# Weights of the first two lanes requested in the routing stage, and the gate row applied by VectorE as the experts' rows leave PSUM

## The chip, the cores and the metric

One Trainium2 chip, one core. The metric is the device time of one execution in microseconds; the median of three executions of the kernel before is 2322.79 us. All data are float32.

## The reference

Two transformer blocks run one after the other on 512 tokens of width 1024. The change touches only the end of the second, its mixture of experts:

```python
scores = sigmoid(hf @ router_w)                     # 512 tokens x 64 experts
choice = scores + router_bias                       # best 4 of 8 groups, then the best 8 experts
gw = scores[top_e] / sum * 2.5
y[token] += swiglu(hf[token], exp_gate[e], exp_up[e], exp_down[e]) * gw      # 8 experts per token
moe = y + swiglu(hf, sh_gate, sh_up, sh_down)       # the shared expert
x = x + g2 * moe                                    # g2: the gate row, 1024 numbers
return rms_norm_2(x, final_g)
```

An expert has a gate and up matrix of 1024x256 each ("gu", 2.10 MB together) and a down matrix of 256x1024 ("down", 1.05 MB). How many tokens an expert gets is known only once the routing has run.

## The kernel before

The program is a list of phases; each is a block in which the five engines run their own instruction streams, and the next block begins when all engines have left the last one. Three phases matter.

**Routing** (`phase_route`). VectorE works through a chain of some 200 small operations, each waiting for the one before. It picks each token's 8 experts (until L2635), assigns experts to blocks of 128 rows (until L2710, `guests_done`), computes each token's place (`slot_f`, L2732 to L2754), then the two rows of numbers from which the weights are fetched: `K.source[:, 0]`, the block's own expert (L2758 to L2763), and `K.source[:, 1]`, a "visitor" expert that uses 32 of the block's 128 rows (L2765 to L2775). After these it builds one-hot tables `within` (L2787, four operations of 128x1024) and `place` (L2790, 32 operations of 128x96), from which TensorE makes the token lists (L2557). Beside that the shared expert runs: TensorE multiplies gate and up (L2522) and down (L2565, eight products of 128x512, through PSUM banks 6 and 7 in turn), ScalarE copies each product out (L2581), and GpSimd adds them to the residual `K.res` (L2591). GpSimd has multiplied the shared down matrix with the gate row before (L2588).

**Experts** (`phase_experts`). 42 blocks are worked off in 14 trips of three lanes (0, 1, 2). Each lane has one buffer for gu and one for down, each with room for an own expert and a visitor. GpSimd gathers the tokens' rows (L2982) and the weights (L2994) by indirect DMA; a lane's gu buffer is refilled once the gu products of its last block are done, the down buffer once its down products are. GpSimd's order at the start is: rows of block 0, weights of lane 0, rows of block 1, a wait for `weigh_step` (12 operations of VectorE, L2966 to L2968), rows of block 2, weights of lane 1, rows of block 3, weights of lane 2, and so on. Nothing is fetched where the block's expert is that of the lane's block before. VectorE transposes the rows (L2947, 16 operations a block); TensorE multiplies gu (L2872 and L2874), then the down product of the block before, then transposes the hidden rows (L2906). ScalarE makes the silu (L2921), VectorE multiplies with the up half (L2958). The finished block leaves PSUM by halves: ScalarE copies columns 0 to 511 (L2916), VectorE columns 512 to 1023 (L2953); SyncE stores it to `expert_out`.

**Combine** (`phase_combine`). Per token 8 rows of `expert_out` are gathered by 32 indirect DMAs (L3050), one for each of 4 token tiles and 8 choices, into 16 buffers. VectorE sums three of the eight with their weights (L3078, L3076), TensorE the other five through diagonal matrices into PSUM (L3063). VectorE adds both sums (L3081), multiplies with the gate row (L3084), adds the residual (L3085), and the final norm follows: ScalarE squares (L3099) and takes the root (L3101), VectorE scales (L3090).

## Time and profile before

| | us |
|---|---|
| median of three executions (2322.01 to 2322.91) | 2322.79 |
| the profiled execution's own time | 2324.35 |
| its span, first to last instruction | 2322.0 |
| TensorE matmul busy | 2089.7 (90%) |
| VectorE busy | 1276.3 (55%) |
| ScalarE busy | 450.4 (19%) |
| GpSimd busy | 428.5 (18%) |
| mean granted TensorE clock | 0.958 |

The routing lies at about 1609 to 1688 us of the span, the experts at 1688 to 2256, the combine at 2256 to 2322. A time in a row is microseconds from the start of the span. Idle time ahead of an instruction stands in brackets with what ended it; idle time of an engine that nobody waits for costs nothing.

### The profile page before, as it was taken

The page shows a single profiled execution, that of the slowest core. Times are in us where ns is not written, and L with a number is a line of the kernel's source. Part 1 is how long each engine was busy: PE and PEld are TensorE (multiplying, and loading weights), DVE is VectorE, ACT ScalarE, POOL GpSimd, SP SyncE. Part 2 cuts the span into 40 slices and gives each one's busy share as a digit, 9 for nine tenths or more (in the row PEclk, how much of TensorE's full clock was granted, in tenths as well). Part 3 has the DMA queues.
Part 4 walks back from the last instruction along what each step waited for, and adds up shares of the span by engine and source line. Part 5 has one row for each costly group of instructions (what it writes and reads, how often), then busy time and mean ns, then how long its engine had stood idle before and what let it go on. Part 6 is the DMA issues. An engine that isn't in the chain of part 4 may idle for free. (4 is left out here: it accounts for less than half of the span.)

```text
span 2322.0 us, 32745 instructions
## 1 busy us (share of the span) xinstructions
PE 2089.7 (90%) x12785; PEld 1214.8 (52%) x12786; DVE 1276.3 (55%) x2404; ACT 450.4 (19%) x889; POOL 428.5 (18%) x779
## 2 busy tenths in 40 slices
PE   6999999999999999999978999898748889989866
PEld 3444564787786448884453598545423333332322
DVE  3347872666663124433977433434865666767635
ACT  1013562212211011002335323101000011101111
POOL 0005000112000000000000000000154555556525
PEclk9999999999999999999989999998879999999988
DMA  9412000545524114991102100401079999998967
GB/s 386 188 65 99 37 1 3 234 147 215 218 96 169 54 63 157 399 363 70 46 1 111 56 2 3 182 37 64 0 322 379 379 424 406 360 402 329 412 270 313
DMA packets 71163, 433.13 MB, mean 187 GB/s; under 512 B 16227, under 2 KB 16883, under 8 KB 46993
## 3 DMA queue, kind: packets, MB, share of 16 engines
q0 software_dynamic: 39488, 245.00, 26.6%
q1 hardware_dynamic: 31570, 186.65, 20.8%
q8 instruction: 76, 1.25, 0.2%
q14 instruction: 29, 0.24, 0.0%
HBM read 462.47 MB, written 68.73 MB: 229 GB/s over the span
## 5 line engine op out<-in xcount | busy, mean ns | idle before, releaser
L2872 PE MATMUL psum<-arena 128*32 128x512 f32 x3024 | 464.3, 618 | 80.8 <-DMA arena<-in_exp_gu,arena 79.9
L2874 PE MATMUL psum<-arena 128*32 x1008 | 463.3, 618 | 0.0
L965 PE MATMUL psum<-arena 128*128 128x256 f32 x1904 | 416.9, 381 | 3.3 <-PEq L1005 2.0
L965 PEld LDWEIGHTS psum<-arena 128*128 128x128 f32 x1904 | 361.3, 190 | 64.2 <-issue 15.3
L2947 DVE STREAM_TRANSPOSE arena<-arena 32x256 f32<-32x256 f32 x688 | 299.6, 435 | 17.8 <-DMA arena<-scratch_h,arena 9.0
L2872 PEld LDWEIGHTS psum<-arena 128*32 128x32 f32 x3024 | 131.6, 114 | 331.6 <-issue 310.9
L1067 PE MATMUL psum<-arena 128*128 128x512 f32 x352 | 151.8, 592 | 0.3 <-PEq L1091 0.3
L2874 PEld LDWEIGHTS psum<-arena 128*32 128x32 f32 x1008 | 110.8, 113 | 7.2 <-issue 3.5
L869 PE MATMUL psum<-arena 128*128 128x512 f32 x256 | 111.2, 593 | 2.3 <-DVE arena L2432 1.5
L1067 PEld LDWEIGHTS psum<-arena 128*128 128x128 f32 x352 | 66.6, 190 | 83.4 <-issue 83.4
L420 DVE SCALAR_TENSOR_TENSOR arena<-arena 128x512 f32<-128x512 f32 x120 | 94.8, 834 | 5.8 <-PEq L456 4.5
L2921 ACT ACTIVATE arena<-psum 128x256 f32<-128x256 f32 x42 | 16.1, 384 | 394.2 <-PE psum L2874 394.2
L2994 POOL DMA_INDIRECT arena<-in_exp_gu,arena x84 | 84.9, 1011 | 37.0 <-issue 37.0
L2994 POOL DMA_INDIRECT arena<-in_exp_down,arena x84 | 85.1, 1013 | 34.9 <-issue 34.9
L2953 DVE COPY arena<-psum 128x512 f32<-128x512 f32 x42 | 29.1, 692 | 109.7 <-PE psum L2874 109.7
L869 PEld LDWEIGHTS psum<-arena 128*128 128x128 f32 x256 | 48.1, 190 | 61.2 <-issue 58.9
L1200 DVE SCALAR_TENSOR_TENSOR arena<-arena 128x511 f32<-128x511 f32 x88 | 68.2, 774 | 15.9 <-ACT arena L1164 13.6
L1164 ACT ACTIVATE arena<-arena 128x512 f32<-128x512 f32 x44 | 33.5, 807 | 217.4 <-DVE arena L984 217.4
L1600 PE MATMUL psum<-arena 128*128 128x512 f32 x128 | 66.6, 652 | 9.1 <-ACT arena L1700 7.1
L244 PE MATMUL psum<-arena 128*32 128x512 f32 x384 | 51.3, 656 | 25.8 <-DMA arena<-in_w_ada 25.8
L972 DVE TENSOR_TENSOR arena<-arena,psum 128x512 f32<-128x512 f32 x34 | 23.4, 687 | 88.8 <-PE psum L965 88.8
L978 DVE TENSOR_TENSOR arena<-arena,psum 128x512 f32<-128x512 f32 x34 | 23.4, 688 | 83.3 <-PE psum L965 83.2
(572 smaller groups left out, 2929.9 us busy)
## 6 DMA issues: line engine op xcount, KB each, us to landing
scratch_expert_out<-arena SPq DMA_DIRECT2D x18, 2048.0 KB, 19.9
arena<-in_w_ada SPq DMA_DIRECT2D x12, 2048.0 KB, 16.8
arena<-in_ada_w POOLq DMA_DIRECT2D x12, 2048.0 KB, 8.1
arena<-in_w_up SPq DMA_DIRECT2D x22, 1024.0 KB, 4.8
scratch_expert_out<-arena SPq DMA_DIRECT2D x42, 512.0 KB, 7.7
arena<-in_w_in SPq DMA_DIRECT2D x9, 2048.0 KB, 11.3
arena<-in_w_down SPq DMA_DIRECT2D x5, 2048.0 KB, 7.8
arena<-in_w_o SPq DMA_DIRECT2D x2, 2048.0 KB, 8.0
```

Source lines behind the costliest of these rows:

```text
L244: last = pe.matmul(bank[32 * j:32 * j + 32, :], vec[:, k, :], w[:, 512 * k:512 * k + 512], start=(r == 0), stop=(r == 1))
L420: K.tap.by(dve.scalar_tensor_tensor(out=conv[:, k, :], in0=x, scalar=w, in1=conv[:, k, :], op0=ALU.mult, op1=ALU.add))
L869: last = pe.matmul(K.bank[2 * t + half], lhs[:, k, P * t:P * t + P], row(k)[:, 512 * half:512 * half + 512], start=(k == 0), stop=(k == pe ...
L965: last = pe.matmul(out, w[:, k, :], x[:, k, :], start=(k == 0), stop=(k == KH - 1))
L1067: out = pe.matmul(K.bank[2 * t + half], K.hmid[:, k, P * t:P * t + P], w[:, k % 4, 512 * half:512 * half + 512], start=(first and k == inn ...
L1164: seed.by(act.activation(conv(n)[half], rows(n)[:, half, :], ACT.Identity, bias=taps[:, n, 4 * half + 3:4 * half + 4], scale=taps[:, n, 4 ...
L1200: link(dve, dve.scalar_tensor_tensor(out=c[:, to], in0=u[:, fr], scalar=taps[:, n, 4 * half + tap:4 * half + tap + 1], in1=c[:, to], op0=A ...
L1600: last = pe.matmul(K.bank[6 if m == 0 else 7], K.gw[:, m % 2, P * k:P * k + P], K.h[:, k, :], start=(k == 0), stop=(k == KD - 1))
L2872: pe.matmul(bank[r, :], left[:, r], weights[:, OWN, col:col + 512], start=first, stop=last_)
L2874: return pe.matmul(bank[0:GUEST, :], left[:, 0:GUEST], picked, start=first, stop=last_)
L2947: last = dve.transpose(channels[c:c + 32, :, a:a + 32], tokens[a:a + 32, :, c:c + 32])
L2994: pool.indirect_dma_start(to[s][:, who, :], None, src, offset, bounds_check=EXPERTS * P - 1, oob_is_err=False).then_inc(landed_[s].sem, 16)
```

## The change

- In the routing VectorE computes the own experts' numbers right behind `guests_done`, then the shared expert's product for half 0, the first part of the ranks, the product for half 1, the visitors' numbers, and only then the places. TensorE's turned table of block experts (`eb_t`) goes to bank 2 and ahead of the last gate-and-up product.
- GpSimd requests the weights of lanes 0 and 1, own experts and then visitors, eight indirect DMAs in all, as soon as the numbers are there; lane 1 waits for the last gate-and-up product, whose buffers it takes. Down buffers of lanes 1 and 2 now lie in the two weight-stream buffers. In the experts' phase GpSimd's order begins with rows of blocks 0 and 1, the same wait for `weigh_step`, rows of blocks 2 and 3, then weights of lane 2.
- The shared expert's eight down products use six banks; VectorE adds each from PSUM to the residual (eight operations of 128x512). ScalarE's eight copies and GpSimd's four adds are gone.
- `place` is made by four operations of 128x768 on VectorE, and scaled by the token numbers in four operations of ScalarE, where 32 operations did both.
- The gate row for the shared expert is loaded in the phase before.
- In the experts' phase VectorE moves both halves out, each multiplied with a gate row loaded at the phase's start; ScalarE moves none.
- In the combine VectorE sums its three rows straight onto the residual and adds the PSUM sum: three operations of one kind and one of another per tile, where there were six. The gate row's load is gone.

```diff
+            K.gate_in.by(pool.dma_start(K.row[:, 3, :], d["mod_rows"][3].partition_broadcast(P)), 16)
...
-    shared, gate_row = sb("shared", [P, NT, D]), sb("route_gate_row", [P, D])
+    down_at = K.ws_taken + 1
+    gate_up_ws, shared_down_ws = K.ws[:, 1 - down_at % 2, :], K.ws[:, down_at % 2, :]
+    K.memory.release("h")
+    K.e_gu = [None] * UNROLL
+    for lane in (1, 0):
+        K.e_gu[lane] = sb(f"e_gu{lane}", [P, 2, KD * 2 * E_FF])
+    K.e_down = [sb("e_down0", [P, 2, 2 * D])] + [x.rearrange("p (w n) -> p w n", w=2) for x in (gate_up_ws, shared_down_ws)]
+    K.e_gu_in, K.e_down_in = ([sig(f"{n}{s}") for s in range(UNROLL)] for n in ("e_gu_landed", "e_down_landed"))
+    gate_row = K.row[:, 3, :]
...
+            eb_t.by(pe.matmul(K.bank[2][:, P:2 * P], K.ones[:, :], diag[:, :], start=True, stop=True))
...
-            for n in range(2 * NT):
+            def down_products(n):
                 t, half = divmod(n, 2)
-                if n >= 2:
-                    pe.wait_ge(sh_out.sem, n - 1)
+                if n == 5:
+                    pe.wait_ge(ranks_read.sem, 1)
+                if n >= len(down_banks):
+                    pe.wait_ge(added.sem, n - len(down_banks) + 1)
                 for k in range(2):
-                    last = pe.matmul(K.bank[6 + n % 2], act_h[:, k, P * t:P * t + P], w[:, k, 512 * half:512 * half + 512], start=(k == 0), stop=(k == 1))
+                    last = pe.matmul(K.bank[down_banks[n % len(down_banks)]], act_h[:, k, P * t:P * t + P], w[:, k, 512 * half:512 * half + 512], start=(k == 0), stop=(k == 1))
                 dn_mm.by(last)
+
+            for n in range(6):
+                down_products(n)
+            list_products(0)
+            list_products(1)
+            down_products(6)
+            down_products(7)
             free(K, dn_mm)
-            for t in range(NT):
-                last = list_products(t)
-            list_mm.by(last)
+            list_products(2)
+            list_mm.by(list_products(3))
...
-            for n in range(2 * NT):
-                t, half = divmod(n, 2)
-                act.wait_ge(dn_mm.sem, n + 1)
-                sh_out.by(act.activation(shared[:, t, 512 * half:512 * half + 512], K.bank[6 + n % 2], ACT.Copy))
+            for t in range(NT):
+                act.wait_ge(matched.sem, t + 1)
+                numbered.by(act.activation(place[:, t, :, :], place[:, t, :, :], ACT.Copy, scale=const[:, RC_TOKEN + t:RC_TOKEN + t + 1]))
 
         @block.gpsimd
         def _(pool):
+            gu_rows, down_rows = d["exp_gu"].rearrange("e p n -> (e p) n"), d["exp_down"].rearrange("e p n -> (e p) n")
+
+            def fetch(lane, who):
+                row = bass.IndirectOffsetOnAxis(ap=K.source[:, who, LANE * lane:LANE * lane + 1], axis=0)
+                for to, src, landed in ((K.e_gu, gu_rows, K.e_gu_in), (K.e_down, down_rows, K.e_down_in)):
+                    landed[lane].by(pool.indirect_dma_start(to[lane][:, who, :], None, src, row, bounds_check=EXPERTS * P - 1, oob_is_err=False), 16)
+
             pool.wait_ge(K.ws_landed[down_at % 2].sem, 16 * (down_at // 2 + 1))
-            pool.wait_ge(gate_in.sem, 16)
+            pool.wait_ge(K.gate_in.sem, 16)
             for k in range(2):
-                gated.by(pool.tensor_tensor(shared_down[:, k, :], shared_down[:, k, :], gate_row[:, :], ALU.mult))
-            for t in range(NT):
-                pool.wait_ge(sh_out.sem, 2 * t + 2)
-                added.by(pool.tensor_tensor(K.res[:, t, :], K.res[:, t, :], shared[:, t, :], ALU.add))
+                gated.by(pool.tensor_tensor(shared_down[:, k, :], shared_down[:, k, :], gate_row, ALU.mult))
+            pool.wait_ge(own_ready.sem, 1)
+            fetch(0, 0)
+            pool.wait_ge(gu_mm.sem, 4)
+            fetch(1, 0)
+            pool.wait_ge(guest_ready.sem, 1)
+            fetch(0, 1)
+            fetch(1, 1)
...
+            at_first = lambda ap: ap[:, 0:BLOCKS].rearrange("p (l t) -> p l t", l=UNROLL)[:, :, 0]
+            dve.wait_ge(eb_t.sem, 1)
+            step(dve.tensor_copy(src_f[:, :], K.bank[2][:, P:2 * P]))
+            step(tt(again[:, 1:P], src_f[:, 1:P], src_f[:, 0:P - 1], ALU.is_equal))
+            step(dve.memset(at_first(again), 0.0))
+            step(ts(at_first(src_f), at_first(src_f), EXPERTS - 1.0, None, ALU.min))
+            step(ts(src_f[:, :], src_f[:, :], float(P), const[:, RC_ROW:RC_ROW + 1], ALU.mult, ALU.add))
+            link(dve, stt(out=K.source[:, 0, :], in0=again[:, 0:BLOCKS], scalar=NOWHERE, in1=src_f[:, 0:BLOCKS], op0=ALU.mult, op1=ALU.add), own_ready)
+
             def shared_product(m):
                 dve.wait_ge(sg_act.sem, m + 1)
                 dve.wait_ge(gu_mm.sem, m + 3)
                 sh_mul.by(tt(act_h[:, m, :], hg[:, m, :], K.bank[6 + m], ALU.mult))
+
+            shared_product(0)
...
+            shared_product(1)
...
+            link(dve, stt(out=K.source[:, 1, :], in0=again[:, 0:BLOCKS], scalar=NOWHERE, in1=src_f[:, 0:BLOCKS], op0=ALU.mult, op1=ALU.add), guest_ready)
...
+            link(dve, tt(tmp[:, :, :], rank, spread_e(limit), ALU.is_ge), ranks_read)
...
+            def add_shared(n):
+                t, half = divmod(n, 2)
+                x = K.res[:, t, 512 * half:512 * half + 512]
+                dve.wait_ge(dn_mm.sem, n + 1)
+                added.by(tt(x, x, K.bank[down_banks[n % len(down_banks)]], ALU.add))
+
             for t in range(NT):
-                low = part[:, 0, TOP * t:TOP * t + TOP].unsqueeze(2).to_broadcast([P, TOP, P])
-                step(tt(within[:, t, :, :], count.unsqueeze(1).to_broadcast([P, TOP, P]), low, ALU.is_equal))
-                for j in range(TOP):
-                    n = TOP * t + j
-                    last = ts(place[:, t, j, :], count[:, 0:BLOCKS], part[:, 1, n:n + 1], const[:, RC_TOKEN + t:RC_TOKEN + t + 1], ALU.is_equal, ALU.mult)
-                    if j < TOP - 1:
-                        r_step.by(last)
-                dve.wait_ge(r_step.sem, r_step.n)
-                link(dve, last, hot)
+                low, high = (part[:, a, TOP * t:TOP * t + TOP].unsqueeze(2).to_broadcast([P, TOP, n]) for a, n in ((0, P), (1, BLOCKS)))
+                link(dve, tt(place[:, t, :, :], count[:, 0:BLOCKS].unsqueeze(1).to_broadcast([P, TOP, BLOCKS]), high, ALU.is_equal), matched)
+                link(dve, tt(within[:, t, :, :], count.unsqueeze(1).to_broadcast([P, TOP, P]), low, ALU.is_equal), hot)
+                if t == 1:
+                    add_shared(0)
+                    add_shared(1)
+            for n in range(2, 2 * NT):
+                add_shared(n)
...
-                act.activation(out[:, (s - 1) % U, 0:512], K.bank[5], ACT.Copy).then_inc(out_act.sem, 1)
...
-                dve.tensor_copy(out[:, (s - 1) % U, 512:D], K.bank[6]).then_inc(out_dve.sem, 1)
+                if isinstance(i, int) and i == 0 and s == 1:
+                    dve.wait_ge(gate_in.sem, 16)
+                for half in range(2):
+                    last = dve.tensor_tensor(out[:, (s - 1) % U, 512 * half:512 * half + 512], K.bank[5 + half], gate[:, 512 * half:512 * half + 512], ALU.mult)
+                last.then_inc(out_dve.sem, 1)
...
-                if isinstance(i, int) and i + s == 0:
-                    weights(i, s)
-                    gather(i, s, 1)
-                else:
-                    if isinstance(i, int) and i == 0 and s == 1:
-                        pool.wait_ge(weigh_step.sem, 3 * NT)
-                        link(pool, pool.memset(xg[U - 1], 0.0), cleared)
-                    gather(i, s, 1)
+                if isinstance(i, int) and i == 0 and s == 1:
+                    pool.wait_ge(weigh_step.sem, 3 * NT)
+                    link(pool, pool.memset(xg[U - 1], 0.0), cleared)
+                gather(i, s, 1)
+                if not (isinstance(i, int) and i == 0 and s < EARLY):
                     weights(i, s)
...
+            gate_in.by(sp.dma_start(gate[:, :], d["mod_rows"][3].partition_broadcast(P)), 16)
...
-                    if j:
-                        dve.wait_ge(used.sem, used.n)
-                        used.by(dve.scalar_tensor_tensor(out=s, in0=yg[:, n % RING, :], scalar=K.weight[:, t, j:j + 1], in1=s, op0=ALU.mult, op1=ALU.add))
-                    else:
-                        used.by(dve.tensor_scalar(s, yg[:, n % RING, :], K.weight[:, t, 0:1], None, ALU.mult))
-                dve.wait_ge(used.sem, used.n)
+                    link(dve, dve.scalar_tensor_tensor(out=x, in0=yg[:, n % RING, :], scalar=K.weight[:, t, j:j + 1], in1=x, op0=ALU.mult, op1=ALU.add), used)
                 dve.wait_ge(summed.sem, ON_PE * (t + 1))
-                first.by(dve.tensor_tensor(gated[:, :], s, banks(t), ALU.add))
-                dve.wait_ge(first.sem, first.n)
-                dve.wait_ge(row_in.sem, 32)
-                link(dve, dve.tensor_tensor(gated[:, :], gated[:, :], gate_row[:, :], ALU.mult), K.dve_step)
-                link(dve, dve.tensor_tensor(x, x, gated[:, :], ALU.add), x3)
+                link(dve, dve.tensor_tensor(x, x, banks(t), ALU.add), x3)
...
-            row_in.by(sp.dma_start(gate_row[:, :], d["mod_rows"][3].partition_broadcast(P)), 16)
```

## Rows read from the trace of the kernel before

**Rows 1.** Stretches: bounds, length, busy us of each engine, clock, DMA share, GB/s
```profile
1650.00:1688.00 38.00, 26.85 (x96) 17.23 (x96) 33.54 (x86) 4.78 (x8) 10.23 (x4) 0.82 0.00 1
...
1742.00:1760.00 18.00, 12.83 (x98) 6.93 (x98) 9.59 (x22) 1.26 (x3) 7.76 (x19) 0.91 1.01 417
...
1796.00:1804.00 8.00, 8.00 (x80) 2.34 (x73) 6.35 (x15) 0.39 (x1) 5.71 (x11) 1.00 0.42 120
```

**Rows 2.** Timeline, TensorE, first gu product of blocks 0, 2, 3, 4: start, us
```profile
1707.92 1.07 PE L2872 MATMUL psum<-arena 128*32 128x512 f32 x3 [20.27 <-DMA arena<-in_exp_gu,arena]
...
1742.53 0.63 PE L2872 MATMUL psum<-arena 128*32 128x512 f32 x3 [3.54 <-DMA arena<-in_exp_gu,arena]
...
1760.38 1.05 PE L2872 MATMUL psum<-arena 128*32 128x512 f32 x3 [5.02 <-DMA arena<-in_exp_gu,arena]
...
1772.95 0.63 PE L2872 MATMUL psum<-arena 128*32 128x512 f32 x3
```

**Rows 3.** Timeline, VectorE, the routing behind `guests_done`
```profile
1646.99 0.20 DVE L2718 TENSOR_SCALAR arena<-arena 128x64 f32<-128x64 f32 x1
...
1651.01 0.22 DVE L2732 TENSOR_TENSOR arena<-arena,psum 128x64 f32<-128x64 f32 x1
...
1655.84 1.28 DVE L2715 TENSOR_TENSOR arena<-arena,psum 128x512 f32<-128x512 f32 x2
...
1658.73 0.29 DVE L2758 COPY arena<-psum 128x128 f32<-128x128 f32 x1
...
1660.38 0.14 DVE L2765 MEMSET arena<- 128x96 f32 x1
...
1663.20 0.14 DVE L2776 TENSOR_SCALAR arena<-arena 1x1 int32<-1x1 f32 x1
...
1663.81 2.33 DVE L2783 CAST arena<-arena 128x64 f32<-128x64 uint32 x1
...
1687.79 0.26 DVE L2797 TENSOR_SCALAR arena<-psum 128x96 uint32<-128x96 f32 x1 [2.22 <-PE psum L2557]
```

**Rows 4.** Groups by line, 1650 to 1780 us: count, busy us, mean ns
```profile
L2790 DVE TENSOR_SCALAR arena<-arena 128x96 f32<-128x96 f32 x32 | 14.0, 511 | 0.1
...
L2787 DVE TENSOR_TENSOR arena<-arena 128x1024 f32<-128x1024 f32 x4 | 4.9, 1225 | 0.3
```

**Rows 5.** Timeline, TensorE, the shared down products and the first list product
```profile
1657.27 16.05 PE L2565 MATMUL psum<-arena 128*128 128x512 f32 x32 [7.46 <-DVE arena L2715]
1673.60 2.02 PE L2557 MATMUL psum<-arena 128*128 128x96 f32 x16 [0.28 <-DVE arena L2790]
```

**Rows 6.** Timeline, GpSimd: first add, gu request of lane 0, rows of block 2
```profile
1663.73 2.35 POOL L2591 TENSOR_TENSOR arena<-arena 128x1024 f32<-128x1024 f32 x1 [45.84 <-ACT arena L2581]
...
1693.93 1.05 POOL L2994 DMA_INDIRECT arena<-in_exp_gu,arena  x1 [0.57 <-issue]
...
1709.55 1.04 POOL L2982 DMA_INDIRECT arena<-scratch_h,arena  x1 [0.51 <-issue]
```

**Rows 7.** Timeline, GpSimd, one request of the combine
```profile
2288.65 1.75 POOL L3050 DMA_INDIRECT arena<-scratch_expert_out,arena  x1 [0.30 <-issue]
```

**Rows 8.** Timeline, VectorE, one move out of PSUM in the experts' loop
```profile
1783.52 0.69 DVE L2953 COPY arena<-psum 128x512 f32<-128x512 f32 x1 [2.60 <-PE psum L2874]
```

**Rows 9.** Groups by line, 2256 to 2322 us
```profile
L3076 DVE SCALAR_TENSOR_TENSOR arena<-arena 128x1024 f32<-128x1024 f32 x8 | 10.3, 1284 | 1.3 <-DMA arena<-scratch_expert_out,arena 0.5
...
L3078 DVE TENSOR_SCALAR arena<-arena 128x1024 f32<-128x1024 f32 x4 | 3.0, 748 | 11.2 <-DMA arena<-scratch_expert_out,arena 11.2
```

**Rows 10.** Timeline, TensorE, the combine
```profile
2268.74 19.24 PE L3063 MATMUL psum<-arena 128*128 128x512 f32 x40 [16.03 <-DMA arena<-scratch_expert_out,arena]
...
2300.66 9.14 PE L3063 MATMUL psum<-arena 128*128 128x512 f32 x20 [2.62 <-DMA arena<-scratch_expert_out,arena]
```

**Rows 11.** Timeline, VectorE, the last tile of the combine
```profile
2314.47 1.22 DVE L3085 TENSOR_TENSOR arena<-arena 128x1024 f32<-128x1024 f32 x1
...
2317.67 1.28 DVE L3090 SCALAR_TENSOR_TENSOR arena<-arena 128x1024 f32<-128x1024 f32 x1
```

More of the change, by code:

```diff
@@ L2743, in _ @@
-            for t in range(NT):
-                step(dve.max(slot_f[:, t, :], tmp[:, t, :]))
-            shared_product(0)
-            shared_product(1)
-            sf = slot_f[:, :, :].rearrange("p t j -> p (t j)")
-            step(ts(num[:, 10:11], N, float(BLOCK), 0.5, ALU.mult, ALU.add))
-            step(ts(num[:, 11:12], N, float(2 * BLOCK), 0.5, ALU.mult, ALU.add))
-            step(ts(num[:, 13:14], N, -float(BLOCK), float(LANE * BLOCK), ALU.mult, ALU.add))
-            step(ts(beyond[:, :], sf, num[:, 10:11], num[:, 13:14], ALU.is_gt, ALU.mult))
@@ L2752, in _ @@
-            step(ts(again[:, 0:NT * TOP], sf, num[:, 11:12], num[:, 13:14], ALU.is_gt, ALU.mult))
-            step(tt(beyond[:, :], beyond[:, :], again[:, 0:NT * TOP], ALU.add))
-            link(dve, stt(out=K.slot[:, :], in0=sf, scalar=-1.0, in1=beyond[:, :], op0=ALU.add, op1=ALU.add), slots_done)
-            at_first = lambda ap: ap[:, 0:BLOCKS].rearrange("p (l t) -> p l t", l=UNROLL)[:, :, 0]
-            dve.wait_ge(eb_t.sem, 1)
-            step(dve.tensor_copy(src_f[:, :], K.bank[3][:, P:2 * P]))
@@ L2759, in _ @@
-            step(tt(again[:, 1:P], src_f[:, 1:P], src_f[:, 0:P - 1], ALU.is_equal))
-            step(dve.memset(at_first(again), 0.0))
-            step(ts(at_first(src_f), at_first(src_f), EXPERTS - 1.0, None, ALU.min))
-            step(ts(src_f[:, :], src_f[:, :], float(P), const[:, RC_ROW:RC_ROW + 1], ALU.mult, ALU.add))
-            step(stt(out=K.source[:, 0, :], in0=again[:, 0:BLOCKS], scalar=NOWHERE, in1=src_f[:, 0:BLOCKS], op0=ALU.mult, op1=ALU.add))
             guests = K.bank[3][:, 3 * P:3 * P + BLOCKS]
@@ L2809, in phase_experts @@
     OWN, VISITOR = 0, 1
-    gu, down = [], []
-    for lane in range(U):
-        gu.append(sb(f"e_gu{lane}", [P, 2, KD * 2 * E_FF]))
-        down.append(sb(f"e_down{lane}", [P, 2, 2 * D]))
-    xt, out = sb("e_xt", [P, U, D]), sb("e_out", [P, U, D])
-    g, ht, xg2 = sb("e_g", [P, U, E_FF]), sb("e_ht", [P, E_FF]), sb("e_x", [P, 2, D])
+    EARLY = 2
+    K.e_gu[U - 1] = sb(f"e_gu{U - 1}", [P, 2, KD * 2 * E_FF])
+    gu, down = K.e_gu, K.e_down
+    K.memory.release("ones", "cols")
+    xt, gate, out = sb("e_xt", [P, U, D]), sb("e_gate_row", [P, D]), sb("e_out", [P, U, D])
+    g, xg2, ht = sb("e_g", [P, E_FF]), sb("e_x", [P, 2, D]), sb("e_ht", [P, E_FF])
     xg = [xg2[:, 0, :], xg2[:, 1, :], K.weigh[:, :]]
@@ L2820, in phase_experts @@
     gu_ready, down_ready = sig("e_gu_rows_ready"), sig("e_down_rows_ready")
-    gu_in, down_in = ([sig(f"{n}{s}") for s in range(U)] for n in ("e_gu_landed", "e_down_landed"))
+    gu_in, down_in = K.e_gu_in, K.e_down_in
     out_dma = [sig(f"e_out_stored{s}") for s in range(U)]
@@ L3022, in step @@
                 sp.dma_start(dst, out[:, s, :]).then_inc(out_dma[s].sem, 16)
+            gate_in.by(sp.dma_start(gate[:, :], d["mod_rows"][3].partition_broadcast(P)), 16)
             steps(sp, step)
-    K.memory.release("slot_f", "r_weigh", "e_xt", "e_x", "e_g", "e_ht", "e_out", "e_rows", "e_weight_rows", "e_wait_for",
-                     *(f"e_gu{lane}" for lane in range(U)), *(f"e_down{lane}" for lane in range(U)))
+    K.memory.release("slot_f", "r_weigh", "e_xt", "e_gate_row", "e_x", "e_g", "e_ht", "e_out", "e_rows", "e_weight_rows", "e_wait_for",
+                     *(f"e_gu{lane}" for lane in range(U)), "e_down0", "ws")
 def phase_combine(nc, K, ctx):
@@ L3038, in phase_combine @@
     row_in, used, x3, squared, ms, root, done, stored = (sig(n) for n in ("final_landed", "c_used", "x3", "x3_squared", "x3_ms", "x3_root", "out_ready", "out_stored"))
-    diag_in, summed, first = sig("c_diagonal_ready"), sig("c_summed"), sig("c_sum_read")
+    diag_in, summed = sig("c_diagonal_ready"), sig("c_summed")
     on_pe = lambda n: n % TOP >= ON_DVE
@@ L3056, in _ @@
                 if t >= 2:
-                    pe.wait_ge(first.sem, t - 1)
+                    pe.wait_ge(x3.sem, t - 1)
                 for j in range(ON_PE):
```

83 lines of the change are left out of this document (43 added, 40 removed).

## The prediction

> **What bounds the kernel now.** I read the busy times by stretch first, then TensorE's timeline, then those of VectorE and GpSimd around the routing's end. In the routing's last 38 us the DMA queues move nothing (share 0.00, 1 GB/s), while VectorE is busy 33.5 us of them; once the experts run, the queues are full (share 1.01 at 417 GB/s), and at one place in the loop they are half empty again (0.42, 120 GB/s, with TensorE busy all 8 of 8 us) [rows 1]. So this stretch has three limits in turn. First VectorE's chain: nothing else can end the routing. Then the weights: TensorE's first gu product waits 20.27 us for them, those of blocks 2 and 3 wait 3.54 and 5.02 us, and only block 4 starts without a wait, at 1772.95 [rows 2]. From there TensorE sets the pace, with waits for weights again later. In the combine the gathered rows and TensorE's products on them come first, VectorE's chain behind them.
>
> **Part 1, the routing.** Up to `guests_done` (1646.99) nothing on VectorE's chain changes. Behind it the pieces change order. Own numbers take 1660.38 - 1658.73 = 1.65 us, so GpSimd may request lane 0's own weights at 1648.6. Then come one shared product (half of 1.28, 0.64), the first part of the ranks (1651.01 - 1646.99 = 4.02), the other product (0.64) and the visitors' numbers (1663.20 - 1660.38 = 2.82): visitors are known at 1656.8 [rows 3]. The sum of the pieces is as before, so the conversion of the digits (CAST) still starts at 1663.8.
> The conversion took 2.33 us for 128x64 elements, from 1663.81 to 1666.14, while a copy of 128x128 takes 0.29 [rows 3]. GpSimd's first add ran from 1663.73 to 1666.08 [rows 6]: VectorE got through only when it ended. GpSimd's adds go, so I set 0.2 (gain 2.1; none if something else held it).
> Next the one-hot tables. Before, 14.0 us for 32 `place` operations and 4.9 for four `within` [rows 4]. Now four `place` operations of 128x768, bounded by 0.64 for 512 elements [rows 3] and 1.225 for 1024 [rows 4]: 0.93. With 0.035 between operations this is 4 x (0.93 + 1.23 + 0.07) = 8.9 us. The eight adds from PSUM cost 8 x 0.67 = 5.4 (0.64 [rows 3] and 0.69 [rows 8] bound one). VectorE is through at 1664.0 + 8.9 + 5.4 = 1678.3.
> TensorE beside it: the down products can start at 1653.9, when both halves are there, against 1657.27. Eight took 16.05 us [rows 5], so six are done by 1666.0; two lists (2.02 each [rows 5]) behind the second `within` at 1668.5 end at 1670.6, two more down products at 1674.6, two more lists at 1678.7. ScalarE's numbering (under 1 us a tile) is hidden behind `within`. VectorE's last operation (0.26) comes behind both: the routing ends at 1679.0 against 1688.05 [rows 3], 9.0 us earlier. The earlier multiplication of the down matrix on GpSimd may move a VectorE operation by up to the 2.1 us of the conversion, either way; I take 0.
>
> **Part 2, the early fetch.** Lanes 0 and 1 hold own expert and visitor each, by the rates: between block 2's and block 3's start, 17.85 us [rows 2] at 417 GB/s [rows 1] are 7.4 MB, which fits down of lane 2 and gu of lane 0, both with visitor (2.10 + 4.19), a gather and a store (0.52 each). So 2 x 6.3 = 12.6 MB move into the routing. At 417 GB/s that is 30 us, from about 1650 to 1681, in a stretch where the queues are empty. The rows of block 0 are asked for about 1682, behind it. I take this as hidden: lane 0's weights are needed at about 1694, lane 1's some 12 us later, and for each microsecond beyond that TensorE waits one.
> Eight requests of 1.05 us each [rows 6] stand on GpSimd between 1648.6 and 1662. Behind them on its queue is nothing of the routing. Beside them VectorE works; a request beside VectorE took up to 1.75 us [rows 7]. For what they hold up on VectorE I take 0.5 us, between 0 and 8 x 1.05 = 8.4.
> Now who is late next. Block 0 starts as soon as its rows are transposed, some 14 us earlier, block 1 behind it without a wait. Then it is lane 2. Its request stands behind `weigh_step` and two gathers. The gather of block 2 moves from 1709.55 [rows 6] to 1700.5, one more gather takes 2.0 us, and the gu request goes out at about 1705.0. Before, the first gu request was at 1693.93 [rows 6] and the product on it at 1707.92 [rows 2]: 13.99 us from request to product with an empty queue. Block 2 thus starts at 1719.0 (TensorE is free for it at 1719), where it was 1742.53. Block 3's gu arrives 17.85 us later, as before and with the same loads between: 1736.8 instead of 1760.38. That is 23.6 us earlier, and 12.57 us later [rows 2] block 4 starts, again without a wait. From there every trigger is tied to TensorE's progress, and the queues run half empty once before the next wait for weights [rows 1], so nothing of the 23.6 is given back. They contain the 9.0 of part 1. A check by rate: between block 0's start and block 3's gu, 21 MB had to come (three gu, three downs with visitors, four gathers); now 7.4 MB come behind block 2's. 13.6 MB at 417 GB/s are 33 us, less the 11.1 us by which the first request in this phase goes out later (1693.93 to 1705.0): 22.
>
> **Part 3, the loop.** VectorE waits 2.60 us in each block before its move out of 0.69 [rows 8]. Now it makes two operations there, one half each: 1.38 us if a multiplication with a row costs what the copy does (0.64 for two operands [rows 3]). The wait shrinks to 1.9; nothing is behind it but the transposes of the next rows, which TensorE needs only after its next down product. Cost 0, were the wait gone 42 x 0.69 = 29. After the last block nothing hides it: 0.6 us. ScalarE's part of the move ran beside VectorE's and gives nothing.
>
> **Part 4, the combine.** Per tile two operations of 1.22 us [rows 11] plus their gaps go (2.5), and one of 0.75 becomes one of 1.28 [rows 9] (0.6 with its gap); in the first tile that one is hidden. VectorE alone: 4 x 2.5 - 3 x 0.6 = 8.2. But TensorE's last sum is ready at 2300.66 + 9.14 = 2309.8 [rows 10]. One addition of 1.25, then from the end of the old last addition (2314.47 + 1.22 = 2315.69) to the end of the last scaling (2317.67 + 1.28 = 2318.95) 3.26 us [rows 11]: 2314.3, that is 4.6 earlier. The gate row's load of 0.52 MB, in front of the gathers, goes as well: 1.25 us at 417 GB/s, of which I count 1.0, between 0 and 1.25. Together 5.6.
>
> **The sum.** 23.6 - 0.5 - 0.6 + 5.6 = 28.1 us. Against the profiled execution (span 2322.0, own time 2324.35) that is a span of 2293.9 and a time of 2296.3; the median of before lies 1.56 below that time, so 2294.7.
>
> **A rule of the skill.** The conversion that ended when GpSimd's add ended [rows 3, 6] shows one engine shutting out the other. The Trainium skill ("SBUF — State Buffer", section "SBUF: two separate sides") says why: VectorE and GpSimd share a pair of ports as an exclusive lock, whoever starts first keeps it for the whole instruction. The same section warns that requests issued by GpSimd can be kept from writing their descriptors by VectorE. By that rule the adds' removal is worth its full 2.1 us, as summed; and it speaks against the early requests, the second rival below.
>
> **Rivals.**
> *Given back (chance 0.08).* The queues bound the whole loop, and TensorE's lead only lengthens the later waits. For it: 417 GB/s over whole blocks; against it the 120 GB/s stretch [rows 1]. Left would be 9.0 + 5.6 - 1.1 = 13.5: 2309.3.
> *Requests and chain shut each other out (0.12).* Each early request costs VectorE its full length, 8.4 us instead of 0.5, or, stretched to 1.75 us [rows 7], delays the transfers and with them the rows of block 0 by as much. For it: the conversion; against it: GpSimd's requests read almost nothing. 2294.7 + 7.9 = 2302.6. That the early fetch does less than it says (visitors absent, a lane's request late) ends here too.
> *More (0.13).* Lane 2's and lane 0's weights come in less than 17.85 us (6.8 MB without the store are 16 at 417 GB/s), the gathers of the combine also speed up, so that more of the 8.2 us counts: 1.8 + 3.6 more, 2289.3.
> *Slower (0.03).* VectorE becomes the bound of the loop. It has 0.69 + 2.60 = 3.29 us a block for both halves [rows 8], so the point is 1.65 us for one. At 2.33 (what an operation took that GpSimd held, [rows 3]) it is 42 x (4.66 - 3.29) = 57.5 too much: 2352. Against it: the nearest rows say 0.64 to 0.69. From 1.98 each on it would be slower than before.
>
> **Chances and range.** Forecast 0.64, rivals 0.08, 0.12, 0.13, 0.03. The range 2286 to 2304 takes in the forecast's unknowns (conversion 2.1, gate row 1, requests up to 8) and two rivals, and leaves out the first and the last, and tails. A change under 0.2%, 4.6 us, can't be told from none. Faster 0.95, same 0.02, slower 0.03.
>
> **What would show it.** GpSimd's requests for lanes 0 and 1 at about 1649 to 1662 and the queues full until 1681; the conversion at about 0.2 us; the routing's last operation at about 1679; gu products of block 0 at 1694, block 2 at 1719, block 3 at 1737, block 4 at 1749; VectorE's two multiplications 0.65 to 0.7 each and a wait near 1.9 before them; the loop's blocks as far apart as before where nothing waits for weights. The forecast is wrong if block 4 is early and the last block is not, if a multiplication takes over 1.65, or if the last tile of the combine still waits for VectorE alone.

## The result, and the profile after

The changed kernel takes 2302.6 us (median of 4 runs, 2298.46 to 2305.69) against 2322.83 of the kernel before on the same chip: ratio 0.9913, 95% interval 0.9895 to 0.993. It is faster, as forecast, but by 20.2 us and not by 28.1. Run again on another chip (`a1_again`, below) it gave 2299.55. Its profiled execution has a span of 2303.7 us (own time 2305.69), where the prediction had 2293.9: 9.8 us to explain. That execution is the slowest of its four; by the medians the gain is 7.9 us short of the forecast (20.2 of 28.1), in the second run 4.8 (2299.55 against 2322.89 on its chip).

The stretches around the routing's end, after (columns as in [rows 1]: length, busy time of PE, PEld, DVE, ACT and POOL with instructions, granted clock, DMA share, GB/s):

```profile
1645.00:1660.00 15.00, 11.35 (x28) 5.14 (x27) 13.38 (x47) 0.00 (x0) 6.04 (x6) 0.89 0.57 223
1660.00:1675.00 15.00, 14.54 (x62) 8.53 (x61) 14.10 (x29) 3.74 (x4) 2.03 (x3) 1.00 1.01 426
1675.00:1690.00 15.00, 3.11 (x28) 2.94 (x27) 7.73 (x13) 0.00 (x0) 4.29 (x7) 0.73 0.63 240
1690.00:1705.00 15.00, 6.08 (x44) 2.36 (x48) 11.85 (x24) 0.00 (x0) 1.66 (x4) 0.59 0.10 31
```

The empty queues of [rows 1] are full from 1660 to 1675, as forecast. The surprise is the last line: 31 GB/s for 15 us (0.10 of the DMA engines' time), in which TensorE first waits for rows and then works off the weights fetched early.

VectorE's timeline after, end of the routing and start of the next phase:

```profile
1664.33 0.19 DVE L2812 CAST arena<-arena 128x64 f32<-128x64 uint32 x1
1664.55 0.96 DVE L2824 TENSOR_TENSOR arena<-arena 128x768 f32<-128x768 f32 x1
1665.55 1.22 DVE L2825 TENSOR_TENSOR arena<-arena 128x1024 f32<-128x1024 f32 x1
...
1674.75 3.67 DVE L2820 TENSOR_TENSOR arena<-arena,psum 128x512 f32<-128x512 f32 x6
1678.35 0.25 DVE L2833 TENSOR_SCALAR arena<-psum 128x96 uint32<-128x96 f32 x1
1684.45 0.69 DVE L2997 TENSOR_TENSOR arena<-arena 128x512 f32<-128x512 f32 x1 [5.86 <-PEq L2522]
```

Part 1 came out: the conversion takes 0.19 us (2.33 in [rows 3]), and the routing ends at 1678.6 (forecast 1679.0). But then VectorE stands still for 5.86 us, and no part of the prediction has that wait. In the kernel before the same wait was 0.54 us long:

```profile
1688.58 0.69 DVE L2966 TENSOR_TENSOR arena<-arena 128x512 f32<-128x512 f32 x1 [0.54 <-PEq L2510]
```

TensorE's gu products after, against [rows 2], then GpSimd's requests (first of the early ones, first gather of block 0, first request of lane 2, which was 1705.0 in the forecast):

```profile
1698.92 1.07 PE L2909 MATMUL psum<-arena 128*32 128x512 f32 x3 [20.82 <-DVE arena L2974]
1741.90 1.08 PE L2909 MATMUL psum<-arena 128*32 128x512 f32 x3 [6.22 <-DMA arena<-in_exp_gu,arena]
```

```profile
1649.71 1.11 POOL L2606 DMA_INDIRECT arena<-in_exp_gu,arena  x1 [35.09 <-DVE arena L2746]
...
1687.26 1.04 POOL L3013 DMA_INDIRECT arena<-scratch_h,arena  x1 [0.52 <-issue]
...
1709.57 1.03 POOL L3025 DMA_INDIRECT arena<-in_exp_gu,arena  x1 [0.54 <-issue]
```

Block 0 now waits for its rows to be transposed and not for weights, and blocks 1 and 2 wait for nothing (before, block 1 had waited 4.67 us for weights at 1726.48, block 2 3.54 [rows 2]). Block 3 waits for weights and starts at 1741.90: 5.1 us after the forecast's 1736.8. Lane 2's request went out 4.6 us after its own forecast.

### The profile page after: what moved, and what is told of

It reads as the page before. It is cut to its first block and busy times, and to the rows that moved or that the text cites. A ratio compares the mean times of both kernels' runs of the same rounds, so it can differ in the third digit from the quotient of the medians.

```text
span 2303.7 us, 32560 instructions
## 1 busy us (share of the span) xinstructions
PE 2082.7 (90%) x12785; PEld 1209.2 (52%) x12786; DVE 1284.4 (56%) x2418; ACT 428.7 (19%) x843; POOL 413.4 (18%) x760
## 5 line engine op out<-in xcount | busy, mean ns | idle before, releaser
L2983 DVE TENSOR_TENSOR arena<-psum,arena 128x512 f32<-128x512 f32 x84 | 54.1, 686 | 95.8 <-PE psum L2911 95.8
L1600 PE MATMUL psum<-arena 128*128 128x512 f32 x128 | 63.7, 626 | 10.8 <-ACT arena L1700 8.8
```

Of the source, the lines that this page charges most:

```text
L1600: last = pe.matmul(K.bank[6 if m == 0 else 7], K.gw[:, m % 2, P * k:P * k + P], K.h[:, k, :], start=(k == 0), stop=(k == KD - 1))
L2983: last = dve.tensor_tensor(out[:, (s - 1) % U, 512 * half:512 * half + 512], K.bank[5 + half], gate[:, 512 * half:512 * half + 512], ALU.mult)
```

## What held the next phase

A DRAIN is the instruction with which each engine ends its part of a block; the next block begins when all have passed it. The trace of the kernel after for the routing's line: each engine's DRAIN (duration in ns, shortest, median and longest, then the start in us) and who waited behind the line.

```profile
L2522 POOLq DRAIN  x1: 25014/25014/25014, 1659.2 to 1659.2; - x1
L2522 ACTq DRAIN  x1: 966/966/966, 1673.5 to 1673.5; - x1
L2522 PEldq DRAIN  x1: 2200/2200/2200, 1676.0 to 1676.0; - x1
...
  DVE arena L2997: 5.9, 1
```

GpSimd's drain takes 25.0 us and ends at 1684.2, where the next phase begins; all others are through by 1678.8. The last early transfers land some 2 us before that end, as the queues' rate shows (stretches of 2 us):

```profile
1680.00:1682.00 2.00, 0.00 (x0) 0.00 (x0) 0.00 (x0) 0.00 (x0) 0.00 (x0) 0.96 0.84 348
1682.00:1684.00 2.00, 0.00 (x0) 0.00 (x0) 0.00 (x0) 0.00 (x0) 0.00 (x0) 0.50 0.09 37
```

In the kernel before, where GpSimd requests nothing in the routing:

```profile
L2510 POOLq DRAIN  x1: 3142/3142/3142, 1674.0 to 1674.0; - x1
```

These 3.1 us are no more than GpSimd's own last addition (3.04 us from 1674.03). The row of VectorE names PE's sequencer as the releaser; PE's own drain was over at 1678.2, so it is not what the phase waited for. The theory: GpSimd's drain at a block's end waits until the transfers that GpSimd requested have landed. The rival: full queues hold the change of phase itself.

## The experiments

A program's start-up differs by up to 5 us between executions (the first early request is at 1649.71 in the profile of after, at 1644.71 in that of `a1_again`, one kernel). Where profiles are compared, times are therefore counted from an event in the same profile.

**The change once more.** 

> The changed kernel once more, unaltered, as the level for the others and to see its scatter (its four executions lay between 2298.5 and 2305.7 us, those of before within 0.9). Both theories: 2302.6 us, scatter of some 7 us again; the routing's last VectorE operation at about 1678.6, the next phase's first at about 1684.4, GpSimd's drain at the block's end about 25 us long. If the scatter lies in the combine, the time from the first gather to the end differs from the 63.0 us of the first profile by some us, and the routing and the first blocks repeat within 0.5 us.

Measured 2299.55 us (2297.31 to 2301.35), ratio 0.9902 [0.9887, 0.9917]; the phase's wait 6.18 us and block 3's wait 7.13 are there again. The changed kernel's level is 2299.6 (chip of this run) to 2302.6 (chip of the first).

**Without the early fetches.**
```diff
-            pool.wait_ge(own_ready.sem, 1)
-            fetch(0, 0)
...
-            fetch(1, 1)
...
-    EARLY = 2
+    EARLY = 0
```


> The changed kernel without the eight early requests; the weights of lanes 0 and 1 are asked for in the experts' phase in the old order. Drain theory (the block's end waits until the transfers that GpSimd has asked for have landed): the wait of 5.9 us behind the routing's last VectorE operation shrinks to the 0.54 of before, block 0 starts at about 1698.5, as early as in the changed kernel, and blocks 2 and 3 at 1733 and 1751; block 3 is thus 9 us later than with the early requests, and the time is 2302.6 + 9 = 2312 us. Rival (the phase change is longer because of the new code or buffers, not because of the transfers): 5.9 us stay, block 3 at 1756, about 2317 us.

Measured 2309.8 us (2304.55 to 2312.57), ratio 0.9941 [0.9927, 0.9955]: the early fetch is worth 10.3 us against the changed kernel on the same chip (2299.55), 7.2 against its first run. Routing and phase change, VectorE:

```profile
1675.97 0.69 DVE L2990 TENSOR_TENSOR arena<-arena 128x512 f32<-128x512 f32 x1 [0.54 <-PEq L2522]
```

The wait is 0.54 us again, and GpSimd's drain is as long as its own two multiplications (4.75 us, 4.69 of them theirs). So the early fetch gives and takes in one place.

This run also prices the requests on VectorE. From the write of the own experts' numbers to the last operation of the routing VectorE takes 29.80 us with the eight requests and 29.51 without. Most of the 0.3 us is one operation that starts beside a request, first after, then without:

```profile
1659.64 0.38 DVE L2791 TENSOR_SCALAR arena<-arena 128x64 f32<-128x64 f32 x1
```

```profile
1656.68 0.19 DVE L2784 TENSOR_SCALAR arena<-arena 128x64 f32<-128x64 f32 x1
```

**Only lane 1's visitor later** (its two requests stand in the first step of the experts' phase, behind the gathers of blocks 0 and 1).
```diff
             fetch(0, 1)
-            fetch(1, 1)
...
+                if isinstance(i, int) and i + s == 0:
+                    K.fetch(1, 1)
```


> As the changed kernel, but the visitor weights of lane 1 (3.1 of 12.6 MB) are asked for behind the first two row gathers of the experts' phase. Drain theory: the early transfers end at about 1674 instead of 1682, GpSimd's drain is over before VectorE, the phase changes 0.5 us behind it, and blocks 0, 2 and 3 start some 5.3 us earlier (block 3 at about 1736.5): 2302.6 - 5.3 = 2297.3 us. Rival (the phase change costs 5.9 us with any early request): no change in block 0's start, 2302.6 us, or slower if lane 1 then waits for its visitor.

Measured 2296.92 us (2296.05 to 2297.91), ratio 0.989 [0.9875, 0.9905], faster than the changed kernel by 2.6 us on the same chip and 5.7 against its first run. Its drain:

```profile
L2522 POOLq DRAIN  x1: 18651/18651/18651, 1657.6 to 1657.6; - x1
```

It ends at 1676.3, ahead of the last operation (1677.91 + 0.25), and the phase's wait is 0.54 us. Six transfers of weights fit in front of the routing's end, eight don't.

**Full queues, but SyncE's** (`e6_sync_traffic`, on the kernel without early fetches).
```diff
+            sp.wait_ge(gu_mm.sem, 4)
+            for n, at in enumerate((14, 18, 22, 26, 46, 50)):
+                dst = d["expert_out"][at:at + 4].rearrange("a (p q) n -> (a p) (q n)", q=4)
+                spare_in.by(sp.dma_start(dst, d["exp_gu"][n]), 16)
```


> The changed kernel without the early fetches, and with traffic of SyncE's instead: six copies of 2.1 MB from DRAM to DRAM, read by nobody, started in the routing and in flight across its end (the time of the whole is worse for it, 10 to 40 us, and says nothing). Theory (the 5.86 us in front of the next phase were GpSimd's drain waiting for its own transfers): with the queues as full but not by GpSimd, the first instruction of the next phase waits about 0.5 us behind the routing's last, as it does with no traffic. Rival (full queues hold the phase change itself, by its code or its semaphores): it waits 4 us or more.

The stretch across the phase change, then VectorE's first instruction behind it:

```profile
1668.00:1676.00 8.00, 6.02 (x38) 4.49 (x36) 7.33 (x12) 1.03 (x2) 0.69 (x1) 1.00 1.11 369
```

```profile
1675.05 0.69 DVE L2999 TENSOR_TENSOR arena<-arena 128x512 f32<-128x512 f32 x1 [0.54 <-PEq L2524]
```

With a DMA share of 1.11, nearly all of it SyncE's copies, the wait is 0.54 us, and SyncE's own drain took 0.37 us with its copies in flight. The rival falls. GpSimd's drain waits for its transfers, SyncE's does not. The two also differ in kind (indirect loads into SBUF against direct copies from DRAM to DRAM), and no run separates the requester from the kind. (Whole time 2316.16 us; it says nothing.)

**Lane 2's weights ahead of the wait for the weighing** (the wait for `weigh_step`).
```diff
                 gather(i, s, 1)
-                if not (isinstance(i, int) and i == 0 and s < EARLY):
+                if isinstance(i, int) and i + s == 0:
+                    weights(0, U - 1)
+                if not (isinstance(i, int) and i == 0):
```


> The changed kernel, with lane 2's first weights requested in step (0,0) right behind the first row gathers, ahead of GpSimd's wait for VectorE's weighing. Theory (the request at 1709.57 is what block 3 waited for, 6.2 us at 1741.90): the request goes out near 1701 to 1702, block 3's wait falls under 1 us, and the kernel is 6 to 8 us faster than the changed one (2299.6 to 2302.6): about 2293.5 us. The wait of 5.9 us of the next phase on GpSimd's drain stays. Rival (the fetches of blocks 3 to 7 are bound by what the queues carry, so an earlier request only moves the wait to block 4 or 5): within 2 us of the changed kernel.

Measured 2293.72 us (2289.36 to 2294.72), ratio 0.9873 [0.9858, 0.9888]. GpSimd's request, and ScalarE's rows at the end of the gu products of blocks 0 to 3:

```profile
1690.72 1.03 POOL L3025 DMA_INDIRECT arena<-in_exp_gu,arena  x1 [0.54 <-issue]
```

```profile
1706.74 0.38 ACT L2952 ACTIVATE arena<-psum 128x256 f32<-128x256 f32 x1 [33.26 <-PE psum L2911]
...
1720.05 0.38 ACT L2952 ACTIVATE arena<-psum 128x256 f32<-128x256 f32 x1 [8.35 <-PE psum L2911]
...
1730.86 0.38 ACT L2952 ACTIVATE arena<-psum 128x256 f32<-128x256 f32 x1 [6.65 <-PE psum L2911]
...
1741.66 0.38 ACT L2952 ACTIVATE arena<-psum 128x256 f32<-128x256 f32 x1 [6.65 <-PE psum L2911]
```

The request goes out 17.9 us earlier, counted from the first early request (I had expected 8), no block waits for weights up to block 3, and from block 1 on the blocks come 10.8 us apart. The phase's wait stays (5.89). Nothing of it is given back later: the last gu product ends 10.5 us ahead of the changed kernel's, both counted from the first early request. What the stretch of 31 GB/s had cost is this request: GpSimd's queue is in order, and it stood behind the wait for all 12 operations of `weigh_step` on VectorE (12.93 us idle in front of 1703.27 in the trace of after), whose result it does not use.

**Both at once.** The edits of "Only lane 1's visitor later" and "Lane 2's weights ahead" together.

> Both at once: lane 1's visitor is requested behind the routing, so that GpSimd's drain has no 10 us of transfer in flight to wait for, and lane 2's weights early in step (0,0). Theory: the phase wait is 0.54 us in place of 5.86 and block 3 waits under 1.5 us; the gains add up to 11 to 13 us on the changed kernel, about 2288.5 us. Rival (one place in the queues: the visitor of lane 1 now lands behind, and pushes lane 2's weights back by its own 10 us): block 3 waits 4 us or more and the time stays at the 2297 of the run with the late visitor alone.

Measured 2287.2 us (2282.14 to 2291.62), ratio 0.9849 [0.9835, 0.9862]; again, with the two below on one chip, 2289.93 (2286.23 to 2293.5), ratio 0.9856 [0.9839, 0.9872]. This is the fastest kernel of the study, 32 to 34 us under the kernel before on the same chip.

> The kernel with both fetches moved, once more beside the next two: 2287.2 us as before, within 3 us. From its first row gather of the combine to the end 62.3 us, the last PSUM sum 54.9 us behind that gather.

The phase's wait is 0.54 us and block 3 has none. Part of the rival holds all the same:

```profile
1709.99 0.38 ACT L2952 ACTIVATE arena<-psum 128x256 f32<-128x256 f32 x1 [7.77 <-PE psum L2911]
1716.86 0.39 ACT L2954 ACTIVATE arena<-psum 128x256 f32<-128x256 f32 x1 [6.49 <-PE psum L2942]
1725.60 0.38 ACT L2952 ACTIVATE arena<-psum 128x256 f32<-128x256 f32 x1 [8.35 <-PE psum L2911]
```

Between blocks 1 and 2 lie 15.6 us in place of 10.8, with the queues at 395 GB/s. What is late is not lane 2's weights but the rows of block 2, gathered behind them and the visitor in the full queues; VectorE waits 7.64 us before it can transpose them:

```profile
1708.70 7.18 DVE L2974 STREAM_TRANSPOSE arena<-arena 32x256 f32<-32x256 f32 x16 [7.64 <-DMA arena<-scratch_h,arena]
```

From the phase's first instruction to the end of block 3's gu product it takes 62.6 us (61.0 in the profile of the second run), 58.1 with lane 2 first alone, 67.0 in the changed kernel. So 3 to 4.5 of what lane 2 gained are paid back to the late visitor, and 5.3 come from the drain.

**The gate edits alone**, on the kernel before (the move out of PSUM by VectorE with the gate row, the short combine). With the three buffers of `g`, the silu's output, this does not fit into SBUF and has no time; the run here has one.
```diff
+                for half in range(2):
+                    last = dve.tensor_tensor(out[:, (s - 1) % U, 512 * half:512 * half + 512], K.bank[5 + half], gate[:, 512 * half:512 * half + 512], ALU.mult)
...
-                first.by(dve.tensor_tensor(gated[:, :], s, banks(t), ALU.add))
...
-                link(dve, dve.tensor_tensor(gated[:, :], gated[:, :], gate_row[:, :], ALU.mult), K.dve_step)
-                link(dve, dve.tensor_tensor(x, x, gated[:, :], ALU.add), x3)
+                link(dve, dve.tensor_tensor(x, x, banks(t), ALU.add), x3)
```


> The gate edits alone, on the kernel before: VectorE takes both halves of a block's output from PSUM times the gate row, and the combine adds rows times weights straight to the residual. Fetches, routing and GpSimd's adds stay as before. My forecast gave the combine 5.6 us less and charged 0.6 us for the start: about 2317.8 us. The profiles of the whole change say otherwise: its last 4.6 us after the last PSUM sum went, but that sum came 1.7 to 3.1 us later after the first row gather, so the first gather to the end is worth 1.4 to 2.8 us and the kernel takes about 2321. The rival in which VectorE bounds the loop of the experts gives more than 2335 us.

Measured 2318.07 us (2315.86 to 2322.91) against 2321.3 of the kernel before on that chip, ratio 0.9985 [0.9974, 0.9996]: a gain of 0.9 to 6.0 us, which separates neither size. The profile does: from the combine's first gather to the end it takes 62.23 us, where the kernel before takes 64.41. Gain 2.2, not 5.6. That is one profile each: in the eight profiles of other kernels with this combine unaltered the distance is 61.6 to 63.3, so the gain is some 1 to 3 us.

**The combine, where its gain went.** Three distances from the first gather, in each profile: TensorE's last tile begins, it ends, the kernel ends. Before: 43.1, 52.2, 64.4 ([rows 10, 11], first gather at 2257.59). After, from 2240.73: 44.8, 55.3, 63.0. The last step shrank from 12.2 to 7.6 us, the 4.6 of the forecast. But the last tile begins 1.75 later and takes 10.52 and not 9.14 us. TensorE and VectorE, after:

```profile
2274.16 8.82 PE L3090 MATMUL psum<-arena 128*128 128x512 f32 x20 [2.67 <-DMA arena<-scratch_expert_out,arena]
2285.55 10.52 PE L3090 MATMUL psum<-arena 128*128 128x512 f32 x20 [2.57 <-DMA arena<-scratch_expert_out,arena]
```

```profile
2248.34 2.61 DVE L3101 SCALAR_TENSOR_TENSOR arena<-arena 128x1024 f32<-128x1024 f32 x2 [0.57 <-DMA arena<-scratch_expert_out,arena]
...
2296.18 1.22 DVE L3103 TENSOR_TENSOR arena<-arena,psum 128x1024 f32<-128x1024 f32 x1 [4.77 <-PE psum L3090]
```

Two suspects. First, GpSimd's requests beside these additions:

```profile
2245.72 0.93 POOL L3077 DMA_INDIRECT arena<-scratch_expert_out,arena  x1 [0.31 <-issue]
2246.96 1.61 POOL L3077 DMA_INDIRECT arena<-scratch_expert_out,arena  x1 [0.30 <-issue]
2248.88 1.55 POOL L3077 DMA_INDIRECT arena<-scratch_expert_out,arena  x1 [0.30 <-issue]
```

```diff
+                if t == 0:
+                    dve.wait_ge(sem_in[10].sem, 16)
```


> The kernel with both fetches moved, and the first tile's three multiply-adds of VectorE in the combine held until row 10 has landed. Theory (these 1.28 us instructions stretch the gather requests that GpSimd writes beside them, so that a transfer is missing some 8 to 16 us behind the first gather): the first 14 requests go out 1.24 to 1.26 us apart with none above 1.0 us long, the queues move 400 GB/s or more from +8 us on, and the last PSUM sum comes 1 to 2 us earlier behind the first gather than the 54.9 us of the run without the hold (53 to 54); the kernel gains 1 to 1.5 us, less than its runs scatter. Rival (the rate hole is the queues' own, from the writes of the experts' last blocks or the number of rows in flight): the hole stays with requests of 0.94 us, and nothing is gained.

Measured 2290.57 us (2288.2 to 2295.11), ratio 0.986 [0.9844, 0.9877], no gain. The stretches from 8 to 16 us behind the first gather, first without, then with the hold, and of the latter GpSimd's last request ahead of the additions and the first beside them:

```profile
2237.53:2245.53 8.00, 6.09 (x10) 2.74 (x11) 1.36 (x2) 0.00 (x0) 6.17 (x7) 0.63 0.85 284
```

```profile
2237.60:2245.60 8.00, 6.01 (x8) 2.70 (x9) 0.00 (x0) 0.00 (x0) 6.03 (x7) 0.53 1.02 400
```

```profile
2248.25 0.93 POOL L3080 DMA_INDIRECT arena<-scratch_expert_out,arena  x1 [0.30 <-issue]
2249.98 1.86 POOL L3080 DMA_INDIRECT arena<-scratch_expert_out,arena  x1 [0.80 <-DVE arena L3106]
```

The mechanism is shown (the last of these rows also waits 0.80 us for the held additions to free its buffer): without additions beside them all 16 requests take 0.93 to 0.95 us and the hole of 284 GB/s is gone. My price for it is not shown: the hold moves the additions, and with them the hole, to 24 to 40 us (381, 360, 395 and 388 GB/s in slices of 4), and the last sum of TensorE comes at 55.9 us behind the first gather, not 53 to 54.

An earlier run says more about the price. With only lane 1's visitor later, the additions happen to fall so that none of the first 16 requests takes over 1.06 us. The same stretch, and the last tile (first gather at 2234.12):

```profile
2242.12:2250.12 8.00, 5.67 (x9) 2.48 (x10) 2.29 (x2) 0.00 (x0) 6.17 (x7) 0.63 1.03 410
```

```profile
2277.53 10.52 PE L3092 MATMUL psum<-arena 128*128 128x512 f32 x20 [3.02 <-DMA arena<-scratch_expert_out,arena]
```

There is no hole, and the last tile begins 43.4 us behind the first gather, 1.4 earlier than in after. So stretched requests are worth about 1.4 us by these two profiles, and operations of VectorE beside a request do not always stretch it.

Second, the clock:

```diff
+                for _ in range(3 if t == NT - 2 else 0):
+                    pe.matmul(K.bank[7], diag[:, 0, 0, :], diag[:, 0, 0:4, :].rearrange("p j k -> p (j k)"), start=True, stop=True)
```


> The kernel with both fetches moved, and three spare 128x512 products of TensorE (about 2.6 us, into a PSUM bank that nobody reads) between the third and the last tile of the combine, where it waits some 3 us for rows. Theory (the last tile's products take 10.52 and not 8.82 us because the granted clock fell in that wait, 0.60 in the 3 us after it): the last tile takes 8.8 to 9.0 us at a clock of 1.0, the end comes 1.5 us earlier behind the first gather, 60.8 us in place of 62.3. Rival (the last tile is slow because its rows land late, not by the clock): it takes 10.5 us all the same.

The last tile in the run with both fetches moved, then with the spare products (its first line):

```profile
2269.38 10.52 PE L3093 MATMUL psum<-arena 128*128 128x512 f32 x20 [3.05 <-DMA arena<-scratch_expert_out,arena]
```

```profile
2271.03 2.74 PE L3097 MATMUL psum<-arena 128*128 128x512 f32 x6
2274.10 8.82 PE L3093 MATMUL psum<-arena 128*128 128x512 f32 x20 [0.33 <-DMA arena<-scratch_expert_out,arena]
```

The last tile takes 8.82 us at a granted clock of 1.00, and from the first gather to the end it is 60.75 us, 62.35 in the profile without: as expected. But in the second profile without, it was the third tile that took 10.52, behind 2.60 us of idle time, the last took 8.82, and the whole 61.97. With the spare products the third tile took 8.82 behind 2.31 us, which they can't have brought about, since they come after it. What they do to the last tile is shown; that they shorten the whole by 1.6 us rests on one profile. The median, 2291.46 us (2287.93 to 2292.99), ratio 0.9863 [0.9847, 0.988], against 2289.93 without: the runs scatter by 5 us, and 1.5 can't be told in them.

## Why the prediction was right in direction and short in size

The direction and the steps of part 1 and part 3 came out by the mechanism forecast. The time lies 7.9 us off, and that it is inside the stated range owes something to luck: what took the 8 us is the mechanism of none of the rivals.

Counted from the profiles, span 2322.0 to 2303.7 is 18.3 us. The first gather of the combine came 16.9 earlier (forecast 22.5) and the rest is 1.4 shorter (forecast 5.6).

- **Part 1, the routing:** right, 9.45 us against 9.0.
- **Requests holding VectorE (0.5), second rival:** the size was about right, 0.3 us by the run without early requests, and far from the rival's 8.4. The time, 2302.6, is the rival's by coincidence. Its last sentence lets a late request of a lane end there too, and lane 2's was 4.6 late, but by the drain, which it does not name.
- **Part 2, "the queues full until 1681; I take this as hidden":** the step that failed. The transfers were hidden from TensorE, which waited for rows, but not from the end of the phase: 5.3 us on everything behind it. Lane 2's request stood behind that (1709.57, not 1705.0), and block 3 came 5.1 late. Requests at 1649 to 1662, full queues until 1681, no wait in blocks 1 and 2 and the next one at block 3 held; the times of the blocks are all late by about the drain (block 0 at 1698.9 and not 1694, block 2 at 1724.8 and not 1719, block 4 at 1755.1 and not 1749). The run with the visitor later shows it, the one with SyncE's traffic says that full queues alone don't do it.
- **"Nothing of the 23.6 is given back":** nearly. From block 3's start to the last gu product the loop takes 484.9 us, 483.9 before: 1.0 lost. Of it 0.65 is block 3's own gu product, which takes 9.52 us at a granted clock of 0.75 behind its wait of 6.22 us, and took 8.87 at 0.81 behind 5.02; the rest is not traced.
- **Part 3:** right. The two multiplications take 1.29 us (forecast 1.38). The wait before them is 1.9 to 2.7 us in all blocks but the last, up to 2.1 in 25 of the 42 (forecast 1.9), and from the last gu product to the first gather it is 13.9 us, 13.3 before (forecast 0.6 more).
- **Part 4:** 4.6 us of VectorE's chain are there. The 1.0 for the gate row shows at TensorE's first tile (10.2 us behind the first gather, 11.15 before) and is gone by the last: TensorE's last sum, which I held fixed, moved by 3.1: 1.75 by rows that came late and 1.4 by the clock. The clock granted in the last tile's first 3 us was 0.57, mostly the lower of TensorE's two levels (1.2 GHz, the upper is 2.4), after a wait of 2.6 us; before, it was 1.00. Of the first, stretched requests are the likely cause (350 GB/s at 8 to 16 us behind the first gather in after, 416 before). The run with the visitor later puts 1.4 us on them, but the hold did not buy it back, so the size is not settled.

The ledger: 5.1 + 1.0 - 0.5 for the start and the loop, 4.2 in the combine, 9.8 in all. Of the 5.1, 0.6 is start-up: VectorE's first instruction of the routing is at 1609.91 after and at 1609.28 before. Counted from it, the routing is 10.1 us shorter, block 3 is 4.5 late and the sum is 9.2; by the profile of `a1_again` the sum is 7.8.

The Trainium skill ("SBUF — State Buffer", section "SBUF: two separate sides") holds GpSimd and VectorE apart by an exclusive lock and warns that VectorE can keep GpSimd from writing its requests' descriptors. The conversion (2.33 to 0.19 us) and the combine's requests (0.94 to 1.5 and 1.9 us beside additions of 1.28) agree. The early requests took 0.98 to 1.11, beside VectorE operations of at most 0.43 us and one of 0.69 with an operand in PSUM, and show no such cost on GpSimd's side.

## What to carry to other kernels

Work moved ahead of a phase's end is hidden only if nothing at that end waits for it: look at how long each engine's drain takes, and whether GpSimd requested what is in flight. On an in-order queue of requests, ask of each wait what stands behind it that doesn't need it; here one such request was worth 6 to 9 us, nearly as much as the early fetch itself. And when the end is cut on one engine, the engine that hands over to it is not a constant: its rows and its clock move with the change.

## Not expected of the hardware

- GpSimd's DRAIN lasts until about 2 us after its own indirect transfers have landed: 25.0 us with eight requests, 18.7 with six. With none it is as long as its last arithmetic, 3.1 and 4.8. SyncE's took 0.37 us with 12.6 MB of its copies in flight.
- A gather request takes 0.93 to 0.95 us alone and up to 1.9 us beside one two-input operation of VectorE of 1.28 us; in one run five requests beside such operations took only 0.93 to 1.06.
- An operation of VectorE can be stretched by a request in turn: 0.38 us in place of 0.19 for 128x64. Eight requests cost VectorE 0.3 us in all.
- A wait of 2.6 us of TensorE between two tiles can lower the granted clock, and doesn't always: behind 2.57 us the last tile of after took 10.52 us, behind 2.67 us the third took 8.82. What decides between them the runs don't show.
